# Multiplications of the identity on TensorE behind layer 0's attention and around the recurrence's first products

## What is computed

```python
def _hgrn2_chunk(S0, xs):
    q, k, v, g = xs
    G = jnp.cumsum(g, axis=1)
    causal = jnp.tril(jnp.ones((T, T), dtype=bool))[None, :, :, None, None]
    decay = jnp.exp(jnp.where(causal, G[:, :, None] - G[:, None, :], -jnp.inf))
    att = jnp.einsum('bthk,btshk,bshk->bhts', q, decay, k)
    o = (jnp.einsum('bhts,bshv->bthv', att, v)
         + jnp.einsum('bthk,bhkv->bthv', q * jnp.exp(G), S0))
    ...
```

## Time and profile before

| | us |
|---|---|
| runs: lowest, median, highest of 3 | 2954.17, 2955.19, 2957.77 |
| profiled execution | 2956.45 |
| its span, first to last instruction | 2954.6 |
| PE busy in the span | 2824.2 (96%) |
| DVE, ACT, POOL busy | 1722.6, 998.7, 1530.0 |
| mean granted clock of TensorE | 0.98 |

### The profile page before, as it was taken

How to read it: one execution, slowest core, us unless ns; L and a number is a source line. 1 busy time by engine, 2 the same in 40 slices (tenths; PEclk the granted TensorE clock), 3 DMA queues, 4 the chain that set the end, 5 groups by cost and what they waited for, 6 DMA issues and landing times. The chain is left out here.

```text
span 2954.6 us, 61044 instructions
## 1 busy us (share of the span) xinstructions
PE 2824.2 (96%) x24967; PEld 2635.7 (89%) x24967; DVE 1722.6 (58%) x3113; ACT 998.7 (34%) x2105; POOL 1530.0 (52%) x1382
## 2 busy tenths in 40 slices
PE   6999999997799999999999999999999999999998
PEld 4869999665699999999999999866699999999998
DVE  6389999556647633436797300066648544346785
ACT  3241111456525333333232201266525333333232
POOL 2222223664524877777576233144334777776675
PEclk8999999997999999999999999999999999999999
DMA  6736762733241122124322232263211222214322
GB/s 222 243 122 227 263 234 74 226 132 120 74 155 51 66 87 83 70 87 139 103 81 75 72 105 96 71 218 102 89 70 41 84 77 76 87 66 138 124 70 70
DMA packets 192389, 339.12 MB, mean 115 GB/s; under 512 B 27992, under 2 KB 107632, under 8 KB 190256
## 3 DMA queue, kind: packets, MB, share of 16 engines
q1 hardware_dynamic: 138832, 266.50, 26.9%
q10 hardware_dynamic: 53280, 68.72, 6.8%
HBM read 268.30 MB, written 79.49 MB: 118 GB/s over the span
## 5 line engine op out<-in xcount | busy, mean ns | idle before, releaser
L758 POOL TENSOR_TENSOR ah_ring_lo<-ah_raw,ah_ring_hi 128x512 fp32r<-128x512 f32 (+2 forms) x426 | 578.7, 1366 | 238.0 <-ACT ah_ring_hi L1182 146.9
L109 PE MATMUL tr_acc<-tr_quad_hi,ah_ring_hi 128*128 128x264 f32 x2432 | 694.5, 286 | 7.7 <-ACT tr_kept L1193 2.6
L111 PE MATMUL tr_acc<-tr_quad_hi,ah_ring_lo 128*128 128x264 f32 x2432 | 693.1, 285 | 0.0
L110 PE MATMUL tr_acc<-tr_quad_lo,ah_ring_hi 128*128 128x264 f32 x2432 | 690.7, 284 | 0.0
L109 PEld LDWEIGHTS tr_acc<-tr_quad_hi,ah_ring_hi 128*128 128x128 f32 x2432 | 458.6, 189 | 9.5 <-ACT tr_kept L1193 3.0
L110 PEld LDWEIGHTS tr_acc<-tr_quad_lo,ah_ring_hi 128*128 128x128 f32 x2432 | 458.6, 189 | 0.1
L111 PEld LDWEIGHTS tr_acc<-tr_quad_hi,ah_ring_lo 128*128 128x128 f32 x2432 | 458.2, 188 | 0.0
L1827 DVE TENSOR_SCALAR_CACHE_REDUCE f_q<-score,choose_trial 128x384 bf16<-128x384 f32 (+6 forms) x224 | 242.2, 1146 | 1.1
L3035 DVE CUSTOM_DVE_ANT_0 pc_prob<-pc_dots,pc_bias 128x640 f32<-128x640 f32 (+4 forms) x128 | 79.0, 655 | 273.3 <-PE pc_dots L2897 272.5
L2151 POOL CAST f_w_hi<-f_raw 128x512 fp32r<-128x512 f32 x66 | 44.5, 675 | 359.9 <-DMA f_raw<-in_w_dram 236.0
L756 POOL CAST ah_ring_hi<-ah_raw 128x512 fp32r<-128x512 f32 (+1 forms) x114 | 72.7, 638 | 279.4 <-PE tr_acc L111 258.6
(11 more groups left out here) (420 smaller groups left out, 7338.7 us busy)
## 6 DMA issues: line engine op xcount, KB each, us to landing
f_ada_w<-in_w_ada_dram SPq DMA_DIRECT2D x48, 1024.0 KB, 7.5
scratch_inner<-tr_kept ACTq DMA_DIRECT2D x88, 264.0 KB, 2.2
ah_raw<-in_w_gate_dram SPq DMA_DIRECT2D x44, 512.0 KB, 3.5
ah_raw<-in_w_up_dram SPq DMA_DIRECT2D x44, 512.0 KB, 4.4
ah_raw<-in_w_down_dram SPq DMA_DIRECT2D x64, 256.0 KB, 3.1
f_raw<-in_w_dram SPq DMA_DIRECT2D x24, 512.0 KB, 9.7
out_z_dram<-f_stage ACTq DMA_DIRECT2D x60, 176.0 KB, 2.0
out_z_dram<-tr_value ACTq DMA_DIRECT2D x48, 176.0 KB, 2.0
```

Source lines behind the costliest of these rows:

```text
L109: pe.matmul(out, w_hi, hi, start=start, stop=False, skip_group_check=onto)
L110: pe.matmul(out, w_hi, lo, start=False, stop=False, skip_group_check=onto)
L111: return pe.matmul(out, w_lo, hi, start=False, stop=stop, skip_group_check=onto)
L758: pool.tensor_tensor(lo[:, 0:width], own, hi[:, 0:width].bitcast(F32), ALU.subtract).then_inc(w_ready, 1)
```

## The change

It adds three groups of multiplications of the identity with itself on TensorE, and nothing else. Their results are never read. 24 go into dots[0] behind pa's last transposition (only where `mask` is given, so not in layer 1's attention). 8 go into the recurrence's turn bank ahead of slot 0 of round 0, and 12 into the same bank between slot 0 and slot 1 of round 0. None waits for a semaphore, and none raises one.

```diff
--- before.py
+++ after.py
@@ -3015,6 +3015,9 @@
                     turns(s - 2, j)
                 if group(s - 4) is not None:
                     side_turn_out(group(s - 4))
+            if mask is not None:
+                for n in range(24):
+                    pe.matmul(dots[0][:, 0:P], ident[:], ident[:], start=True, stop=True)
 
         @block.vector
         def _(dve):
@@ -3798,6 +3801,11 @@
                                              r[:, hd, tile + 64:tile + P], start=True, stop=True)
                 last.then_inc(pairs_done, 1)
 
+            def awake(times):
+
+                for n in range(times):
+                    pe.matmul(turn[:, 0:P], c.ident[:], c.ident[:], start=True, stop=True)
+
             def turn_keys(p):
                 t = tile_at[p]
                 n = t // 3
@@ -3859,8 +3867,12 @@
             for n in range(ROUNDS):
                 if n:
                     turn_keys(3 * (n - 1))
+                if n == 0:
+                    awake(8)
                 for pr in range(2):
                     pairs(n, 0, pr)
+                if n == 0:
+                    awake(12)
                 for at in range(LAST):
                     lv, pr = divmod(at, 2)
                     if lv < LEVELS:
```

## The result

| | before | changed |
|---|---|---|
| median of 6 runs, us | 2954.68 | 2966.15 |
| lowest, highest | 2952.55, 2957.77 | 2960.86, 2969.79 |
| profiled execution, its span | 2956.45, 2954.6 | 2964.61, 2962.7 |

The changed kernel takes 1.0037 times as long, 95% interval 1.0027 to 1.0047, so +8 to +14 us. The forecast was +3.2. It is slower by more than the 0.2% that the prediction named as the bound of no change, and its median lies above the stated range. The later measurement of the same kernel gives 1.0027 (1.0016 to 1.0038), so +5 to +11.

A forecast was written before the change was run, and what follows sets the result against it. It took the recurrence to be bound by a relay of PE, GpSimd and VectorE at half clock, not one engine. 2.8 + 0 + 0.8 - 0.4 = +3.2 us gave 2959.65 profiled, 2958.4 by median; range 2953.5 to 2963.0.

The forecast's parts named there:

- The 24, +2.8: Attention's end: PE's drain waits for the 24 multiplications, holding the barrier from 702.84 to 705.65, +2.8 us.
- One thing it named: Sign at the attention's end: PE's DRAIN gets about 5.4 us longer and ends last.
- The 8, nothing: Ahead of round 0's first pairs: 1.8 us of multiplications, but nobody needs the first set early, cost 0.
- The 12, +0.8: Behind the first pairs: 2.65 us of multiplications delay GpSimd's third scaling, +0.8 us if the 2.20 us wait stays away.
- The clock, -0.4: Round 0: sets at full clock save 0.24 us where GpSimd waits; one or two such waits give -0.4 us.
- 1.00 until some 712: Sign in round 0: the granted clock stays full until about 712.
- 0.50 by about 720: Sign in round 0: the granted clock is down at half by about 720.
- terms 2 to 4: Round 0: the 8 multiplications 0, the 12 multiplications +0.8, the clock's return -0.4 us.
- the one on the fetch: Start of the recurrence: added instructions move the late fetch into filler, the next to where PE waits anyway; no stall cost.
- The rival of a late fetch: The stall moves ahead of level 1's first set, +5.8 us, or some +6.8 with a second short stall; 18%.
- The rival of an idle clock: Identity products don't hold the clock, which falls at 702.7 as before: +10.8 us, 2966.0; 6%.
- The rival of the later dips: Half-clock stretches at 774.5, 798 and 812 could vanish with the shift: -3 us at best, -6 with held clock; 8%.

The follow-up runs named there:

- late load: SyncE's load of w_out waits until the fourth tile is finished: ratio to the kernel before 1.0031 on the changed kernel, 0.9994 on the kernel before.

## Why the prediction was wrong

- **The 24, +2.8: right, 2.87.** Mechanism and size: PE's DRAIN ends last. One thing it named came otherwise: the DRAIN is 2.2 us long and not 5.7, and starts at 705.3, while the passes still run. Its end counts, not its length.
- **The 8, nothing: right.** The first sets end at 711.43, R+3.0.
- **The 12, +0.8: right, 0.9** (third scaling at R+9.5 for R+8.6). No fetch came late in that stretch, as it had said.
- **The clock, -0.4: it fell at 721.1**, later than "1.00 until some 712" and about when "0.50 by about 720" said. The parts of the sum had counted the filler at full clock already; round 0 came out at +1.3 where terms 2 to 4 say +0.4. An effect of the size of -0.4 can't be told here.
- **The step that failed** is the one on the fetch: "the fetch that came late now falls due during the quiet filler, and the next one at about the end of level 1's second set". Both are so. But it stopped there: 176 instructions more ahead of rounds 1 and 2 move every later end of a block too, to the 79th of 96 passes in the densest place of the round, where the wait also drops the clock for the products behind it. That term was not in the sum, and it is 2.3 to 6 us. With the barrier and round 0 it gives 6.5 to 10.2, beside the measured 8 to 14 and 5 to 11.
- **The rival of a late fetch** (18%) had the right agent, and the wrong place and price: it bounded the wait by the one row that it had, 2.20 us ahead of level 1, and foresaw one more of 1 us. There was none ahead of level 1, and the one in round 2 was 3.9. The rival of an idle clock came near in time (2966.0) by luck; its mechanism did not happen. The rival of the later dips had the sign wrong: the dip at 774.3 comes at 775.8, as long as before (6.8 us), but now over the dense products of round 2; the one at 798 has none beside it, one at 768.9 is new, and the last comes at 820.1 for 811.8. Its own sentence that they "can as well get longer" is the nearest that the prediction came to this; this one covers the dense passes between slots 1 and 2 now (2.4 us) and not those between slots 3 and 4 (0.4 us).
- **The quoted rule** of the Trainium skill ("Runtime: NRT & Kernel Launch", section "Instruction fetch mechanics"), that the stream comes in blocks of 256 and that the crossing is "mostly hidden": the first half is what all traces show; the second holds for most ends (in the change 4 of the 16 ends from R to the start of the tail carry a wait of 0.4 us or more), and fails by 3.9 us where PE takes a whole block in a burst. The prediction used the rule for the next end only, where its first half, followed through three rounds, named the danger.

The first lines of this trace could have given it: the waits for issue at R+6.2, 10.0, 18.8, 36.4, 50.3, 63.1 and 69.4 are all at one remainder. With the number of added instructions known, the new places follow by counting; what they cost could not have been read from this trace; over the runs the recurrence came out 3 us shorter to 7 us longer.

## What to carry to other kernels

Adding instructions to an engine that runs short ones in bursts moves the end of every later block of 256; count where the ends fall in all the rounds behind an edit, not only beside it, before crediting or blaming the edit itself. Try an edit in a form that has the same number of instructions and no work, and a filler of a few cheap instructions at an idle place, to tell the two apart: here one-column multiplications, which are hardly any work, made -3 to +6.5 us of a 110 us stage. Read a second trace before a price is put on a wait, since the same code gave 0.99 us in one and 2.92 in the other. When a wait appears, look at what runs behind it as well: here the granted clock fell during the wait, and the 24 dense passes that followed took 2.4 us longer for it. Work that keeps TensorE's clock up must fit under what holds the barrier; 5.5 us of it under 2.6 us of cover cost its excess to the last tenth.

## What was not expected of the hardware

- A wait for issue of 3.6 to 4.1 us with the core's DMA nearly idle (late load) as well as busy: the packet of the instruction queue itself takes 0.9 to 1.5 us, and PE goes on 2.2 to 2.9 us behind its start. In the changed kernel's round 2 it started 3.1 us behind PE's step into the block before (5.4 us from one end to the next), in the kernel before 0.6 us behind it (2.8 us). What sets that start was not settled.
- The same code in the same place has the wait in one execution and not in the other: round 1 of the change, 0.99 and 2.92 us, 33.0 and 35.6 us for the round.
- A product of one column and its weight load of 128x1 take PE 0.03 us a pass (88 passes in 2.34), so 48 passes, 96 instructions, were free under the 1.75 us of VectorE's product (R stayed 1.02 us behind its end); 128 passes moved R by 0.8.
